# Row totals at the block boundaries and at the program's end taken in another order, in a two-block sequence kernel on one Trainium2 core

## What is computed

```python
def rms_norm(x, w):
    return x * lax.rsqrt(jnp.mean(x * x, -1, keepdims=True) + RMS_EPS) * w

for i in range(DEPTH):                        # first block
    mix = gated_deltanet(rms_norm(hs, norm_w[i, 0]), ...) if i % 2 == 0 else mlstm(...)
    hs = hs + keep * rms_norm(mix, norm_w[i, 1])
    f = conv_ffn(rms_norm(hs, norm_w[i, 2]), ...)
    hs = hs + keep * rms_norm(f, norm_w[i, 3])

for l in range(DEPTH):                        # second block
    h = rms_norm_2(x, norm_g[l])
    ...                                       # pooled, attended and memory branches of h @ w_in[l]
    # pooled = trailing-window mean (2, 4, 8, 16 tokens, one per group of channels) - the token
    # logits of the attention get a bias, rel_bias[rel_bucket(key - query)]
    x = x + merged @ w_out[l]
return rms_norm_2(x, final_g)
```

## Time and profile before

| what | value |
|---|---|
| median of 3 runs | 1613.1 us (1612.18 to 1613.17) |
| profiled execution, its own time | 1605.75 us |
| its span | 1603.9 us |
| TensorE busy | 97% |
| VectorE busy | 70% |
| ScalarE busy | 55% |
| GpSimd busy | 22% |
| mean granted TensorE clock | 0.974 of full |

### The profile page before, as it was taken

The page is one execution under the profiler, slowest core; times in us unless marked ns, Lnnn a source line. Parts: engine busy times, 40 slices in busy tenths (PEclk is TensorE's granted clock), DMA queues, the critical chain, the costliest instruction groups (busy, mean ns, idle before and its releaser), DMA issues.

```text
span 1603.9 us, 35080 instructions
## 1 busy us (share of the span) xinstructions
PE 1563.8 (97%) x14221; PEld 1472.2 (92%) x14221; DVE 1118.8 (70%) x2296; ACT 882.6 (55%) x1942; POOL 357.2 (22%) x425
## 2 busy tenths in 40 slices
PE   7999999989999999999999999999999999999998
PEld 6987898969899999988899999989899999898998
DVE  4777777666588864756799976667766666776663
ACT  6665555545466653556386664544554564545554
POOL 4232223404133221001333432000302210030010
PEclk9999999989899998999799999999999999999999
DMA  6322032315365553433355776545346755444552
GB/s 209 120 82 81 28 95 67 95 53 173 97 196 181 172 179 124 144 120 106 115 181 185 197 230 190 179 132 175 111 149 184 224 185 158 146 131 137 154 179 85
DMA packets 64977, 230.42 MB, mean 144 GB/s; under 512 B 7312, under 2 KB 9488, under 8 KB 64816
## 3 DMA queue, kind: packets, MB, share of 16 engines
q1 hardware_dynamic: 59792, 217.67, 43.6%
q0 software_dynamic: 4160, 8.98, 1.9%
q10 hardware_dynamic: 864, 1.52, 0.3%
HBM read 222.91 MB, written 5.24 MB: 142 GB/s over the span
## 4 chain that ended last, share of the span: by engine, by line
PE 84%; DVE 5%; issue 4%; ACT 3%; POOL 3%; DMA 1%; ACTq 0%; SPq 0%; POOLq 0%; DVEq 0%
PE ps L701 81%; PE ps L705 3%; POOL sq L3193 1%; DVE arena L2391 1%; DVE splitL L2383 1%; ACT arena L1803 1%; ACT splitH L1798 1%; DMA ring<-wst 1%; ACT L1803 1%; DVE mixT L2388 1%; DVE mixT L2391 0%; POOL sq L3406 0%; DMA arena<-x 0%; POOL arena L3193 0%; ACT sq L1803 0%
## 5 line engine op out<-in xcount | busy, mean ns | idle before, releaser
L2383 DVE TENSOR_TENSOR splitL<-ring,splitH 128x512 fp32r<-128x512 f32 x767 | 566.0, 765 | 199.7 <-ACT splitH L1798 190.2
L701 PE MATMUL ps<-aH,splitH 128*128 128x256 f32 (+2 forms) x2232 | 662.4, 298 | 9.0 <-ACT aH L1803 5.2
L701 PE MATMUL ps<-aH,splitL 128*128 128x256 f32 (+2 forms) x2232 | 638.8, 287 | 0.0
L701 PE MATMUL ps<-aL,splitH 128*128 128x256 f32 (+2 forms) x2232 | 624.2, 286 | 0.0
L1798 ACT ACTIVATE splitH<-ring 128x512 fp32r<-128x512 f32 x824 | 481.3, 623 | 134.4 <-PE ps L701 121.4
L701 PEld LDWEIGHTS ps<-aH,splitH 128*128 128x128 f32 x2232 | 427.4, 192 | 26.2 <-issue 13.2
L701 PEld LDWEIGHTS ps<-aH,splitL 128*128 128x128 f32 x2232 | 428.0, 192 | 0.0
L701 PEld LDWEIGHTS ps<-aL,splitH 128*128 128x128 f32 x2232 | 419.5, 190 | 0.5
L701 PE MATMUL ps<-arenaR,splitH 128*128 128x256 f32 (+2 forms) x1856 | 350.6, 289 | 1.6 <-ACT arena L1803 1.1
L701 PEld LDWEIGHTS ps<-arenaR,splitH 128*128 128x128 f32 x1856 | 292.7, 192 | 3.1 <-ACT arena L1803 1.6
L701 PE MATMUL ps<-arenaR,splitL 128*128 128x256 f32 (+2 forms) x928 | 265.8, 286 | 0.0
(11 more groups left out here) (203 smaller groups left out, 1337.2 us busy)
## 6 DMA issues: line engine op xcount, KB each, us to landing
ring<-wst SPq DMA_DIRECT2D x412, 512.0 KB, 3.8
mem_scratch<-arenaR POOLq DMA_DIRECT2D x16, 128.0 KB, 3.9
arenaR<-mem_scratch POOLq DMA_DIRECT2D x4, 512.0 KB, 8.7
rel_scratch<-arena POOLq DMA_DIRECT2D x8, 255.5 KB, 5.0
arena<-x SPq DMA_DIRECT2D x2, 512.0 KB, 4.9
arena<-mem POOLq DMA_DIRECT2D x2, 512.0 KB, 4.4
arena<-rel_scratch POOLq DMA_DIRECT2D x1, 1024.0 KB, 10.2
out<-arena ACTq DMA_DIRECT2D x4, 256.0 KB, 2.1
```

Of the source, the lines that this page charges most:

```text
L701: return pe.matmul(out, lhsT, rhs, start=start, stop=stop)
L2383: dve.tensor_tensor(lo, raw, hi.bitcast(F32), ALU.subtract).then_inc(*inc(("lo_dve", q)))
```

## The change

- **Boundaries.** `ADDED` is 6 for "gdn" and "f0" too: POOL adds tile 6, and three tallies stand apart in place of six together. "ml" stays at 5.
- **Order on DVE.** In `add_norm` the first `scale` stands ahead of `second_reciprocal` (gdn, f0 and ml).
- **Order on ACT.** At gdn the high part of j comes ahead of the copy of bias row j, for j = 0 to 2, where all three bias rows came first.
- **Bias products** use 128 rows of weights and table; 96 are zero. `tables` clears `relb` on 128 rows, loads a 128 x 512 one-hot table (32 x 511 before) and then the 32 rows of biases.
- **Pooling on DVE.** Group 0 stays ahead of zm; groups 1, 2 and 3 stand behind steps 1, 6 and 14 of zm.
- **The end.** POOL adds tiles 1 to 6 of the squares of `x1`, and ACT squares tile 7; TensorE's transposes of tile m-1 stand behind block 5 of tile m, the total of tiles 0 to 6 behind the last block, then that of tile 7 and the last two transposes. One root, one reciprocal. ACT calls a dummy square root at tile 0. SP starts the two stores of DVE's half, ACT those of its own.

```diff
-        ADDED = {"gdn": 5, "f0": 5, "ml": 5, "f1": 6}
+        ADDED = {"gdn": 6, "f0": 6, "ml": 5, "f1": 6}
...
-                mm(psum[b][:, :], relH[0:32, h:h + 1].broadcast_to([32, 128]), hotR[0:32, :], True, False)
-                mm(psum[b][:, :], relL[0:32, h:h + 1].broadcast_to([32, 128]), hotR[0:32, :], False, True).then_inc(*inc(("rel", h)))
+                mm(psum[b][:, :], relH[:, h:h + 1].broadcast_to([128, 128]), hotR, True, False)
+                mm(psum[b][:, :], relL[:, h:h + 1].broadcast_to([128, 128]), hotR, False, True).then_inc(*inc(("rel", h)))
...
+                def tokens_of(m):
+
+                    w.wait_ge("xs", m)
+                    for x in range(2):
+                        if m % 4 == 0:
+                            (bg2 if m and x else bg).get("fin", x, m // 4)
+                        t = tr(ps("fin", x, m // 4)[:, m % 4 * 128:m % 4 * 128 + 128], sq[:, m, x * 128:(x + 1) * 128])
+                        if m % 4 == 3:
+                            t.then_inc(*inc(("fin", x, m // 4)))
+
+                for m in range(KD):
                     for k in range(KD):
+                        next(d)
+                        if k == 5 and m:
+                            tokens_of(m - 1)
+                        if k == 7 and m == 7:
+                            first_total(1)
+                        yield
+                for _ in d:
+                    pass
+                last_total(1, ("xsum",))
+                tokens_of(7)
...
                 second_root(mix, i, n)
-                if mix == "gdn":
-                    for h in range(RELS):
-                        biases(h)
-                highs(i, n)
+                for j in range(4):
+                    high(i, j, n)
+                    if mix == "gdn" and j < RELS:
+                        biases(j)
...
                             w.wait_ge("x", l, m)
-                            if m % 4 != 3 or l == 0 and m == 7:
+                            if m == 0 and l:
+                                dummy()
+                            if m != 3:
                                 a(mixT[:, m, 0:N], xT[:, m, :], ACT.Square).then_inc(*inc(("sqa", f"x{l}", m)))
...
+                w.wait_ge("xsum")
+                a(rx[:, 0:2], psum[0][:, 0:2], ACT.Sqrt, bias=V("eps", 0), scale=1.0 / D).then_inc(*inc(("rxs",)))
...
                 energy(mix, n)
+                scale(mix, i, 0, n)
                 second_reciprocal(i, n)
-                scale(mix, i, 0, n)
...
-                yield from gated("zm", zmT)
+
+                pooled(0)
+                yield from beside(gated("zm", zmT), {1: lambda: pooled(1), 6: lambda: pooled(2), 14: lambda: pooled(3)})
...
+                pool.memset(relb, 0.0).then_inc(*inc(("rpad",)))
+                pool.dma_start(hot, arr["hot"]).then_inc(*inc(("rb", 0), by=16))
+                w.wait_ge("rpad")
+                pool.dma_start(relb[0:32, :], arr["rel_bias_2"]).then_inc(*inc(("rb",), by=16))
...
-                            if l == 0 and 1 <= m <= 6:
+                            if 1 <= m <= 6:
...
+            for k2 in range(2):
+                w.wait_ge("find", k2)
+                sp.dma_start(arr["out"][0, 0:128, k2 * 512:(k2 + 1) * 512], fin[:, 0, k2 * 512:(k2 + 1) * 512]).then_inc(*inc(("stored0", k2), by=16))
```

More of the change, by code:

```diff
@@ L76 @@
     ("matt_pe", "mlg mpt mpv mytr"),
-    ("end_pe", "xt sum fin"),
+    ("end_pe", "xt xsum fin"),
     ("end_act", "xs rxs fina"),
@@ new lines, in second @@
+                d = dense(f"x{l}", ("w_out_2", l), [128 * m for m in range(KD)], KD, both(gH, gL, N), N, gneed,
+                          lambda m: [("x", l, m)])
+                if l == 0:
+                    yield from d
+                    return
+                def tokens_of(m):
[6 more added lines that the diff above has]
+                            t.then_inc(*inc(("fin", x, m // 4)))
@@ L1782, in main @@
                 yield from second(1)
-                last()
                 assert feed.u + 1 == NUNIT and feed.col == UNIT, (feed.u, feed.col)
@@ L1814, in high @@
                 a(aH[:, s, 0:n], x[:, s, 0:n], ACT.Copy).then_inc(*inc(("nhi", i, j)))
-            def highs(i, n):
-                for j in range(4):
-                    high(i, j, n)
             def biases(h):
@@ L2324, in last @@
             def last():
-                for x in range(2):
-                    w.wait_ge("sum", x)
-                    a(rx[:, x:x + 1], ps("sum", x)[:, 0:1], ACT.Sqrt, bias=V("eps", 0), scale=1.0 / D).then_inc(*inc(("rxs", x)))
+                w.wait_ge("xsum")
+                a(rx[:, 0:2], psum[0][:, 0:2], ACT.Sqrt, bias=V("eps", 0), scale=1.0 / D).then_inc(*inc(("rxs",)))
                 for k2 in range(2):
-                    for x in range(2):
-                        o_ = fin[:, x, k2 * 512:(k2 + 1) * 512]
-                        if x:
-                            w.wait_ge("rx", 1)
-                            w.wait_ge("fin", 1, k2)
-                            a(o_, ps("fin", 1, k2)[:, :], ACT.Copy, scale=rx[:, 3:4]).then_inc(*inc(("fina", k2)))
-                            w.wait_ge("fina", k2)
-                        else:
-                            w.wait_ge("find", k2)
-                        act.dma_start(arr["out"][0, x * 128:(x + 1) * 128, k2 * 512:(k2 + 1) * 512], o_).then_inc(*inc(("stored", x, k2), by=16))
-                w.wait_ge("stored", 1, 1)
+                    o_ = fin[:, 1, k2 * 512:(k2 + 1) * 512]
+                    w.wait_ge("rx")
+                    w.wait_ge("fin", 1, k2)
+                    a(o_, ps("fin", 1, k2)[:, :], ACT.Copy, scale=rx[:, 3:4]).then_inc(*inc(("fina", k2)))
+                    w.wait_ge("fina", k2)
+                    act.dma_start(arr["out"][0, 128:256, k2 * 512:(k2 + 1) * 512], o_).then_inc(*inc(("stored1", k2), by=16))
+                w.wait_ge("stored1", 1)
             def main():
@@ L2353, in main @@
                 feed.ahead(0)
-                highs("in", T)
+                for j in range(4):
+                    high("in", j, T)
                 feed.ahead(3)
@@ L3079, in second, with pooled @@
                 yield from four_("mq", mqT)
-                for g in range(4):
+                def pooled(g):
                     src, dst = (yb, ya) if g % 2 == 0 else (ya, yb)
@@ L3131, in last @@
             def last():
-                for x in range(2):
-                    w.wait_ge("rxs", x)
-                    dve.reciprocal(rx[:, 2 + x:3 + x], rx[:, x:x + 1]).then_inc(*inc(("rx", x)))
-                w.wait_ge("rx", 0)
+                w.wait_ge("rxs")
+                dve.reciprocal(rx[:, 2:4], rx[:, 0:2]).then_inc(*inc(("rx",)))
+                w.wait_ge("rx")
                 for k2 in range(2):
```

58 lines of the change are left out of this document (18 added, 40 removed).

## The result

| | before | after |
|---|---|---|
| median, runs of the first comparison | 1613.1 us (1612.18 to 1627.4, 7 runs) | 1601.89 us (1596.93 to 1609.77, 7 runs) |
| ratio, 95% interval | | 0.9937 [0.9908, 0.9966] |
| profiled execution, its span | 1603.9 us | 1607.9 us |
| its mean granted clock | 0.974 | 0.965 |

A forecast was written before the change was run, and what follows sets the result against it. TensorE, busy 97% of the span, was taken as the bound. Terms -3.6 - 4.8 - 1.1 - 0.6 + 1.9 - 2.0 - 0.8 = -11.0 us took the 1613.1 us median to 1602.1 us, range 1597.5 to 1609.

The forecast's parts named there:

- tallies gdn and f0, their number: Last tiles of gdn and f0: three of six tallies go, 0.71 us each, 2.1 us per boundary at the high clock.
- the low stretches behind them: Behind the tallies at gdn and f0: the half-clock stretches vanish, saving 1.5 us at each.
- high parts first: Gdn boundary: ACT's earlier high part lets the next product start 1.3 us earlier; -1.1 us (bounds -0.7 and -1.4).
- bias on 128 rows: Gdn's bias products: same own time, but may bring the clock back sooner; 0 to -1.3 us, taken as -0.6.
- scale ahead of the reciprocal: DVE at gdn, f0 and ml: the second reciprocal comes later, a loss of +1.9 us (bounds 0 and +2.4).
- pooling spread: Second block, l = 1: DVE's and TensorE's waits for POOL's last group go; -2.0 us (bounds -3.2 and +2).
- the end: Program end: tail -3.5 us, transposes moved into the product +1.7, table-load wait +1.0; -0.8 us (bounds +0.6 and -1.8).
- the covers: Gdn and f0: POOL's addition of tile 6 is ready in time; no wait charged, up to 1 us if late at gdn.
- The first rival: Gdn and f0: the low clock returns behind the fewer tallies; -6.8 us in all, 1606.3 us, chance 0.18.
- Nothing absorbs it: F0 boundary: the reciprocal's 0.55 us delay passes on in full, since DVE sets the pace from then on.
- The second rival: Pooling: the moved attention tasks wait, giving +2 in place of -2; -7.0 us in all, 1606.1 us, chance 0.11.
- The forecast wait of 1.0 us: Program end, first transposes of x1: TensorE waits while ACT's dummy root loads its table, 1.28 us; +1.0 us.

The follow-up runs named there:

- e1: Kernel before with POOL adding tile 6 at gdn and f0, so three tallies stand apart instead of six together: 1609.86 us, ratio 0.9956.
- e9: Kernel before with POOL adding tile 6 at gdn and f0, the three tallies left together behind block K-2: 1609.51 us, ratio 0.9987.
- e7: Kernel before with only ACT's order at gdn changed, high part j ahead of bias row j: 1613.63 us, ratio 0.9998.
- e10: Kernel before with high parts first at gdn and bias products on 128 rows with larger tables: 1612.08 us, ratio 0.9981.
- e3: Kernel after with the bias products on 32 rows again, tables and all else kept: 1604.6 us, ratio 0.9936 against before.
- e2: Kernel after with DVE's second reciprocal ahead of the first scale again at three boundaries: 1606.01 us, ratio 0.9951 against before.
- e4: Kernel before with only the pooling spread, groups 1 to 3 between zm's blocks: 1615.02 us, ratio 1.0010.
- e8: Kernel after with the old pooling, all four groups ahead of zm's first block: 1604.88 us, ratio 0.9954 against before.
- e5: Kernel before with only the new end of the program: 1611.12 us, ratio 0.9995.
- e6: Kernel before with all six tallies kept at gdn and f0, each alone, two blocks apart: 1615.61 us, ratio 1.0022.

## Why the prediction was right, term by term

At equal clock after is 8.0 ± 0.4 us under before; another 10.0 ± 3.2 us of low clock, 3.6 us, make up the rest of the 11.3 ± 1.2.

| term | sum | measured, at equal clock | by |
|---|---|---|---|
| tallies gdn and f0, their number | -4.2, and -1.1 where they ran at the low level | -4.1 ± 0.7, -4.0 ± 0.4 | e1, e9 |
| the low stretches behind them | -3.0 | -2.1 ± 0.7 (by low us, the 1.1 among it; -0.4 ± 1.2 from e1 and e9 alone) | 79 against 153 executions |
| high parts first | -1.1 | -1.0 ± 0.4 | e7 |
| bias on 128 rows | -0.6 | -1.7 ± 0.6, -3.6 ± 0.6 | e10 less e7, after less e3 |
| scale ahead of the reciprocal | +1.9 | rows +1.8 to +2.7, total -0.8 ± 0.5 | e2 |
| pooling spread | -2.0 | +1.1 ± 0.4, +0.7 ± 0.5 | e4, e8 |
| the end | -0.8 | -1.2 ± 0.5 | e5 |

- **Tallies.** 0.71 us each was right, and the covers held: none waited for POOL. The sum's words "such a stretch costs 16 x 0.097 = 1.5 us ... I take the 1.5 us as saved" were right for the place (both stretches are gone) and too large for the kernel: of 10.2 us of low clock 5.9 went over all runs, and by the profiled executions part of the rest came back at f0's boundary (10.9 us in the mean, where it was 8.5). The reason given, that tallies in a row bring the low clock, fell with e6 and e9. The first rival had the low clock come back behind the tallies; in none of the eight profiled kernels with three did it, up to the end of the product. (The prediction also reads the row loosely: counted from 1, its slices under 9 are 9, 11, 16 and 20. Nothing in the sum rests on it.)
- **The page on the clock.** The sum set a row against the Trainium skill (TensorE: Matmul & The Clock Gate, section HAM oscillation — how this bites in real kernels), which has idle gaps as what brings the low clock. The trace of e6 differs from the page once more: the fall at 408.6 has 6.00 us of busy out of 6.00 ahead of it. It speaks against the sum's own reading of the row too.
- **High parts first** was sized right. **Bias products** were mis-sized: -0.6, the middle of a range without a row; the clock came back about 3 us earlier in five profiles of six, and the term came out at the range's far end or past it.
- **Scale ahead of the reciprocal.** The step itself, 0.55 us at f0, 0.9 at gdn and 0.4 at ml, is in the rows (0.8 to 1.0, 0.7 to 1.0, 0.3 to 0.7), larger than said at f0. "Nothing absorbs it" is what the total contradicts, and it stays open.
- **Pooling** is the step that failed: "I take -2.0 us (bounds -3.2 ... and +2)" took the waits of one execution for the gain. Over the profiled kernels TensorE's idle time there is only 0.3 us less with the new order, and the total is about 1 us worse. The second rival ("the moved attention tasks wait", +2) named the side of the result, at half its price, but new waits alone are not what makes it. After's waits of 1.14 and 0.50 us are 0.9 less than before's, and even that did not reach the total.
- **The end.** The tail was right (4.1 against 4.23). The forecast wait of 1.0 us for the table load did not come: the first transposes start 0.34 us behind the matmul ahead of them, with a usual pitch of 0.12, so 0.2 us. The step that failed there is an overlap: the sum put the load behind the eviction of tile 0, and it started at 1578.67, 0.70 us ahead of that eviction. The load was done at 1579.95 and the scaled copy at 1580.87. The row of the load, 1.28 us with the next activation 0.01 us behind, is the price to go by. The Trainium skill (ScalarE: Activation LUTs, What ACT_TABLE_LOAD costs) gives about 2.66 us with a drain; its figure for the load alone, 1283 ns, agrees with both traces, and the drain shows in neither.

The errors of the terms: tallies +2.2 (6.2 for 8.4), pooling +2.9, bias rows -1.1 to -3.0, end -0.4; together +1.7 to +3.6, while the whole missed by 0.3 (11.3 ± 1.2 for 11.0). So -2 to -4 us lie in what no term accounts for: the order of the reciprocal (-2.7 if e2's total is taken) and 1.5 us of clock beyond the tallies' 2.1 (more, if the tallies' part is less). They nearly cancelled, which is luck. The range of 1597.5 to 1609.0 held both medians of after.

## What to carry to other kernels

Work that leaves the matrix engine where it is always busy pays its own duration, exactly; what it seems to do to the clock besides can be worth less than the rows at that place show (here 5.9 of 10.2 us of low clock by all runs, 8.5 of 10.8 by the profiles), because low stretches come back elsewhere. A wait that is removed by moving work of a planner's is no gain until the whole stretch is measured, in more than one execution: here waits of 1.7 and 0.9 us were traded for others, and about 1 us was lost. Where runs differ by more than the effect, regress the spans on the granted clock before comparing; it cut the error of each difference from 1.5 us to 0.5.

## What was not expected of the hardware

- Six products of 512 columns take 2.90 us on 32 rows and 2.93 on 128, but the clock comes back 2.9 to 3.6 us after the start of those on 128 rows in five profiles of six (6.0 in the sixth), and 6.0 to 10.4 us after those on 32. 96 rows of zeros make no difference to the products' time and one to the clock's.
- The clock fell in a stretch in which TensorE was busy 6.00 of 6.00 us, with tallies two blocks apart at gdn (408.6) and not with the same tallies at f0.
- In identical code the second block took 611.8 and 614.2 us in two profiled executions, and whole executions of after 1594.35 to 1609.77 us.
